# A two-block transformer kernel on one core: gate work, head order and the spatial product rearranged

## The reference, cut to what matters

```
x = first_block(x, ...)      # pool mixer, layer norm, SwiGLU, layer norm
# second block: two layers, each h = h + rmsnorm(mixer(rmsnorm(h)))
# layer 0: differential attention, 8 heads, and a chunked mLSTM, 4 heads
s = where(k_pos <= q_pos, q @ kT, -inf)            # two score maps a head
p = softmax(s); a = p[0] - lam * p[1]; o = a @ v
# mLSTM: log_sigmoid(f), cumulative sums and running maxima over chunks of 128
# layer 1: spatial gating, 8 groups of 256 columns, chunks of 128 tokens
vs = einsum('gts,bcsgd->bctgd', w_spatial * causal, vg) + b_spatial
y = gelu(u) * vs * silu(z);  out = y @ w_out
```

## Time and profile before

| | us |
|---|---|
| Median of 3 runs (2949.52 to 2954.93) | 2954.9 |
| Profiled execution, device time | 2955.26 |
| Its span, first to last instruction | 2953.5 |
| PE busy in it | 2818.0 (95%) |
| PE weight loads busy | 2264.0 (77%) |
| DVE busy | 1359.2 (46%) |
| POOL busy | 1209.1 (41%) |
| ACT busy | 745.6 (25%) |

### The profile page before, as it was taken

The page is one execution under the profiler, slowest core; times in us unless marked ns, Lnnn a source line. Parts: engine busy times, 40 slices in busy tenths (PEclk is TensorE's granted clock), DMA queues, the critical chain, the costliest instruction groups (busy, mean ns, idle before and its releaser), DMA issues.

```text
span 2953.5 us, 38283 instructions
## 1 busy us (share of the span) xinstructions
PE 2818.0 (95%) x14586; PEld 2264.0 (77%) x14586; DVE 1359.2 (46%) x2131; ACT 745.6 (25%) x1218; POOL 1209.1 (41%) x583
## 2 busy tenths in 40 slices
PE   7899999999988899999997999999989999999997
PEld 2588888888867777777775888888778888888885
DVE  6433433343365466555556654645440034444445
ACT  3600000000035333333332222232441322111112
POOL 0544444444335322222221334433254455555555
PEclk9999999999999999999998999999999999999999
DMA  9211111111102100101010111111223311111113
GB/s 386 79 55 45 50 50 43 50 50 45 40 30 87 36 29 28 36 28 36 30 34 15 51 51 50 50 48 52 86 95 106 111 61 57 57 57 57 57 64 122
DMA packets 62900, 185.35 MB, mean 63 GB/s; under 512 B 17108, under 2 KB 23380, under 8 KB 60648
## 3 DMA queue, kind: packets, MB, share of 16 engines
q1 hardware_dynamic: 42016, 152.68, 15.1%
q10 hardware_dynamic: 20808, 31.61, 3.1%
HBM read 163.22 MB, written 21.05 MB: 62 GB/s over the span
## 4 chain that ended last, share of the span: by engine, by line
PE 83%; DVE 7%; ACT 4%; issue 3%; DMA 1%; POOL 1%; DVEq 0%; ACTq 0%; SPq 0%; POOLq 0%
PE ps L711 26%; PE ps L713 25%; PE ps L712 25%; PE ps L1051 2%; DVE acc L2186 1%; PE ps L779 1%; PE ps L1062 1%; DMA resid<-x_t 1%; DVE stat L2337 1%; PE ps L885 1%; PE ps L852 1%; ACT sg_z L1989 1%; DVE da_al L2357 0%; PE ps L1099 0%; ACT ps L1758 0%
## 5 line engine op out<-in xcount | busy, mean ns | idle before, releaser
L538 POOL TENSOR_TENSOR slab_hi<-slab_raw,zero 128x1024 fp32r<-128x1024 f32 x227 | 433.6, 1910 | 1514.8 <-PE ps L713 1408.7
L711 PE MATMUL ps<-h_hi,slab_hi 128*128 128x512 f32 x2256 | 895.4, 397 | 11.8 <-POOL h_lo L554 5.1
L713 PE MATMUL ps<-h_hi,slab_lo 128*128 128x512 f32 x2256 | 883.0, 391 | 0.0
L712 PE MATMUL ps<-h_lo,slab_hi 128*128 128x512 f32 x2256 | 882.4, 391 | 0.0
L540 POOL TENSOR_TENSOR slab_lo<-slab_raw,slab_hi 128x1024 fp32r<-128x1024 f32 x227 | 573.0, 2524 | 17.8
L711 PEld LDWEIGHTS ps<-h_hi,slab_hi 128*128 128x128 f32 x2256 | 425.9, 189 | 111.4 <-issue 14.3
L713 PEld LDWEIGHTS ps<-h_hi,slab_lo 128*128 128x128 f32 x2256 | 425.3, 189 | 91.7
L712 PEld LDWEIGHTS ps<-h_lo,slab_hi 128*128 128x128 f32 x2256 | 426.3, 189 | 84.6
L2186 DVE TENSOR_TENSOR acc<-ps,acc 128x512 f32<-128x512 f32 x352 | 228.7, 684 | 24.5 <-PE ps L713 23.1
L2193 DVE TENSOR_TENSOR ffn_p<-ps,ffn_g 128x1024 f32<-128x1024 f32 x22 | 26.9, 1224 | 454.3 <-PE ps L713 448.7
L2184 DVE SCALAR_TENSOR_TENSOR resid<-ps,mod,resid 128x512 f32<-128x512 f32 x320 | 213.1, 743 | 0.0
(11 more groups left out here) (327 smaller groups left out, 4042.1 us busy)
## 6 DMA issues: line engine op xcount, KB each, us to landing
slab_raw<-w_in SPq DMA_DIRECT2D x168, 512.0 KB, 3.6
mod_big<-mod_w SPq DMA_DIRECT2D x12, 2048.0 KB, 11.2
slab_raw<-w_c SPq DMA_DIRECT2D x43, 512.0 KB, 3.6
res_scr<-resid ACTq DMA_DIRECT2D x4, 2048.0 KB, 7.2
resid<-res_scr ACTq DMA_DIRECT2D x2, 4096.0 KB, 12.9
gv_scr<-sg_t ACTq DMA_DIRECT2D x4, 2048.0 KB, 7.1
slab_raw<-gv_scr SPq DMA_DIRECT2D x16, 512.0 KB, 3.5
resid<-x_t SPq DMA_DIRECT2D x2, 2048.0 KB, 16.1
```

The lines of the kernel that those rows point to most:

```text
L538: pool.tensor_tensor(hi, raw[slot][:], zeros, ALU.add).then_inc(hi_done.sem, 1)
L711: pe.matmul(dst, w_h, r_h, start=first, stop=False, skip_group_check=True)
L712: pe.matmul(dst, w_h, r_l, start=False, stop=False, skip_group_check=True)
L713: return pe.matmul(dst, w_l, r_h, start=False, stop=last, skip_group_check=True)
```

## The change

The spatial weights' high and low parts become one tile of 2 x 8 x 128; a chunk takes one 256-column matmul (the value slab's high part by both) and one 128-column matmul (its low part by the high weights), into 2048 columns of PSUM instead of 1024, and DVE adds the two halves in two passes. `gates(3)` (six of eight chunks) moves into block 0 of head 0, the gate's subtractions on POOL behind one more slab split each for the next head's values and queries, ACT's exponentials ahead of a value copy and the stores behind block 4's exponentials. In the heads, ACT copies block 4's second turned part before the query half and the squares, and the second query half before block 7's exponentials; DVE's order follows. One output addition of block 3 moves between the two maxima. In the norms ahead of attention, tile 2 of half 1 is centred and squared later, and POOL's low split of the slab IN_DA + 1 waits for `mean_square`.

```diff
-        wr_hi, wr_lo = (take(f"sg_{n}", [P, NC, P], F32R)[0] for n in ("wrh", "wrl"))
+        wr_both = take("sg_wrb", [P, 2, NC, P], F32R)[0]
+        wr_hi, wr_lo = (wr_both[:, n, :, :] for n in range(2))
...
+        spatial = ps[:, 2 * T:4 * T].rearrange("p (c h t) -> p c h t", h=2, t=P)
@@ pool: split gets an argument fused, and between its two operations
+                if fused is not None:
+                    pool.wait_ge(n_fuse.sem, fused)
@@
             split_in(IN_DA, 0, IN_DA // 2)
+            split(IN_DA + 1, 1, in_load[1], in_load[1].at((IN_DA + 1) // 2), in_hi, in_mm, in_split, n_fuse.at(0, 2))
             for s in range(1, 8):
-                split_in(IN_DA + s, s % 2, (IN_DA + s) // 2)
+                if s >= 2:
+                    split_in(IN_DA + s, s % 2, (IN_DA + s) // 2)
                 if s == 1:
                     split_low(1, range(2 * KT))
-                if s == 3:
+                if s == 5:
                     gate_exponents()
@@ tensor
                 for c in range(NC):
-                    mm = three(PS[2][:, c * CHUNK:(c + 1) * CHUNK], whi[C][:, c, :], wlo[C][:, c, :],
-                               wr_hi[:, c, :], wr_lo[:, c, :], True, True)
+                    pe.matmul(spatial[:, c, :, :], whi[C][:, c, :], wr_both[:, :, c, :], start=True, stop=False, skip_group_check=True)
+                    mm = pe.matmul(spatial[:, c, 0, :], wlo[C][:, c, :], wr_hi[:, c, :], start=False, stop=True, skip_group_check=True)
@@ scalar: norms
             root_shifted(0)
-            square_centred(1, KT + 2)
             shift(0)
             shift(1)
-            square_centred(1, KT + 3)
+            square_centred(1, KT + 2)
             for k in range(2, KT):
+                split_high(1, k - 2)
+                if k < 7:
+                    square_centred(1, KT + 1 + k)
                 shift(k)
-                split_high(1, k - 2)
-                if k < 6:
-                    square_centred(1, KT + 2 + k)
@@ scalar: gate_rows ends after the exponentials; its wait and five stores are store_gates
@@ scalar: da_head, block i
+                    if i == 6 and not last:
+                        da_q_half(h + 1, 1)
                     if i + 1 < KT:
                         da_exp(h, i + 1)
...
+                    if i in (4, 5):
+                        da_turned(h, i, 1)
+                    if not last and i == 4:
+                        da_q_half(h + 1, 0)
                     if i == 4:
                         da_square(h, 0)
-                    if i == 5:
-                        da_turned(h, i, 1)
...
+                    if i == 2 and first:
+                        gate_rows()
                     if i in (1, 2):
                         da_v_half(h + 1, i - 1)
-                    if not last and i in (4, 6):
-                        da_q_half(h + 1, (i - 4) // 2)
...
-                    if i >= 4 and i != 5:
+                    if i >= 6:
                         da_turned(h, i, 1)
-                    if i == 2 and first:
-                        gate_rows()
+                    if i == 3 and first:
+                        store_gates()
@@ vector: norms
             mean_square(0)
-            center(1, KT + 2)
             gain_first(0)
             reciprocal(2, 0)
             gain_first(1)
-            center(1, KT + 3)
-            gain_first(2)
+            center(1, KT + 2)
             for k in range(KT):
                 layer_input(2, 1, 0, k, "l0_pre_g")
-                if k < 4:
-                    center(1, KT + 4 + k)
                 if k < 5:
-                    gain_first(3 + k)
+                    center(1, KT + 3 + k)
+                if k < 6:
+                    gain_first(2 + k)
@@ vector: da_head
-                        da_max(h, i + 1)
+                        da_max(h, i + 1, (lambda: da_out_add(h - 1, tiles[0], 0)) if out and i == 3 else None)
...
                     if i == 0:
+                        if first:
+                            gates(3)
                         da_turn_low(h, i, 0)
...
-                    if i == 5:
+                    if i in (4, 5):
                         da_turn_low(h, i, 1)
                     if not last and i == 4:
                         da_q_low(h + 1, 0)
...
-            for part in (2, 3):
-                gates(part)
+            gates(2)
             da_k_low(0, 1)
@@ vector: sg_tile, after the first scalar_tensor_tensor, which now reads spatial[:, :, 0, :]
+                dve.wait_ge(e_vs.sem, e_vs.at(d))
+                dve.scalar_tensor_tensor(by_chunk, spatial[:, :, 1, :], gain_col, by_chunk, ALU.mult, ALU.add).then_inc(e_v.sem, 1)
```

More of the change, by code:

```diff
@@ L532, in _, with split @@
             pool.sem_inc(c_split.sem, c_split.prime)
-            def split(n, slot, load, load_value, hi_done, used, done):
+            def split(n, slot, load, load_value, hi_done, used, done, fused=None):
                 pool.wait_ge(load.sem, load_value)
@@ L1660, in gate_rows, with store_gates @@
                 act.activation(g_d3[:], g_d3[:], ACT.Exp).then_inc(g_act.sem, 1)
+            def store_gates():
                 act.wait_ge(g_act.sem, 6)
@@ L2331, in da_out_add, with da_max @@
                 add_half(PS[3], C_DA + h, OUT_DA + h, d, da_halves(d)[n], n=n)
-            def da_max(h, i):
+            def da_max(h, i, between=None):
                 n = (i + 1) * P
                 for c in range(2):
+                    if c == 1 and between is not None:
+                        between()
                     dve.wait_ge(a_score.sem, a_score.at(h, 2 * i + c))
@@ L2420, in da_head @@
                         for d in tiles:
-                            for n in range(2):
+                            for n in range(1 if d == tiles[0] else 0, 2):
                                 da_out_add(h - 1, d, n)
@@ L2659, in sg_tile @@
                 dve.wait_ge(e_yl.sem, e_yl.at(d - 1))
-                dve.scalar_tensor_tensor(sg_v[:].rearrange("p (c t) -> p c t", t=P), PS[2].rearrange("p (c t) -> p c t", t=P),
-                                         par[:, bass.ds(d + COL["sg_g"], 1)],
-                                         bsp[:, bass.ds(g, 1), :].to_broadcast([P, NC, P]), ALU.mult, ALU.add).then_inc(e_v.sem, 1)
+                by_chunk = sg_v[:].rearrange("p (c t) -> p c t", t=P)
+                gain_col = par[:, bass.ds(d + COL["sg_g"], 1)]
+                dve.scalar_tensor_tensor(by_chunk, spatial[:, :, 0, :], gain_col,
+                                         bsp[:, bass.ds(g, 1), :].to_broadcast([P, NC, P]), ALU.mult, ALU.add).then_inc(e_vs.sem, 1)
+                dve.wait_ge(e_vs.sem, e_vs.at(d))
+                dve.scalar_tensor_tensor(by_chunk, spatial[:, :, 1, :], gain_col, by_chunk, ALU.mult, ALU.add).then_inc(e_v.sem, 1)
                 dve.wait_ge(e_v.sem, e_v.at(d))
```

## The result

The changed kernel took 2930.48 us (median of 5 runs, 2925.23 to 2935.02) against 2954.93 us; the ratio is 0.9918, 95% interval 0.9907 to 0.9929. Forecast were 2930.5 us and 2924 to 2938. Timed a second time, beside 2953.48 us for the kernel before, it gave 2934.8 us and 0.9934 (0.9921 to 0.9948); the two medians of one kernel lie 4.3 us apart, and the hit to the tenth is luck. The profiled execution took 2930.48 us (span 2928.7).

What follows compares the result with a forecast made beforehand. PE was taken to bound the kernel, busy 2818.0 of 2953.5 us. Spatial -11.0, heads 1 to 6 -9.6, head 7 -0.9, head 0 -3.5 and norms +0.6 summed to -24.4 us: 2930.5 us, range 2924 to 2938.

Steps and rivals of the forecast that it cites:

- Spatial loop, -11.0: Spatial loop: 0.82 us less in each of 14 tiles, gain of tiles 0 and 1 lost with 0.5 us more; -11.0 us.
- Heads 1 to 6, -9.6: Six loop heads: block 4 gains 0.8, block 6 0.7, the moved addition 0.1; 1.6 us a head, -9.6 us.
- rival 2: Loop heads: gains half absorbed by PE's next wait, 0.8 us a head less; 2935 us, or 2940 if all; chance 0.15.
- (a): Head 0: gate maxima no longer precede the first maximum, so PE's second score map starts at 930.55 instead of 932.42.
- (b): Head 0: moved gate scans meet POOL's split; PE goes on at 942.6, not 940.20, 2.4 us later, after idling 4.5.
- (c): Head 0: lower clock of 1.2 GHz behind the 4.5 us idle stretch, taken as 2.2 us.
- (d): Head 0: gate exponentials and stores moved on ACT; 5.17 us wait shrinks to 0.3, a later one becomes 2.8; -0.9 us.
- (e): Head 0: the two ACT moves, -0.6 and -1.15 us, the last from the 3.13 us wait; lower clock avoided, -0.8.
- Norms, +0.6: Norms ahead of attention: POOL's wait frees the mean 1.0 us earlier, but spread comes later; projection at 869.2, +0.6 us.
- Rival 1: Head 0's opening runs free: scans end before POOL's split or pass it, no lower clock; 2925 us; chance 0.13.
- Rivals 3: Spatial product gains nothing: the 256-column matmul takes two narrow distances; 2942 us; chance 0.04.
- Rival 4: Spatial product slower: the 128-column matmul waits for the wide one's end; 2967 us, deciding from 0.40 us a pair; chance 0.04.

Runs made afterwards that it cites:

- experiment 1: The changed kernel with the old spatial product (24 matmuls of 128 columns, one DVE pass): 2943.59 us, ratio 0.9966.
- Experiment 8: The changed kernel with POOL's split of the second spatial slab ahead of its low part of the first tile: 2925.75 us, ratio 0.9907.
- experiment 4: The changed kernel with all gate work of head 0 in its old places: 2933.03 us, ratio 0.9929.
- experiment 10: The changed kernel itself, unaltered, measured and profiled a second time: 2934.8 us, ratio 0.9934.
- experiment 2: The changed kernel with the old ACT and DVE order in block 4 alone: 2938.18 us, ratio 0.9946.
- 11: The changed kernel with the first output addition behind both maxima of block 4 again, as before: 2932.58 us in one execution.
- Experiment 5: The changed kernel with the old order of centrings, squares, gains and shifts in the norms, POOL's wait for the mean kept: 2932.82 us, ratio 0.993.
- 9: The changed kernel with old norms order, head 0's split behind gate maxima, earlier zeroings, and second spatial slab's split ahead of the low part: 2917.92 us, 0.9881.
- experiment 3: The changed kernel with the second query half behind block 7's exponentials on ACT, as before: 2933.35 us, ratio 0.9928.
- experiment 6: The changed kernel with POOL's split of the next slab in head 0 waiting until DVE's gate maxima are done: 2925.56 us, ratio 0.9905.

## Why the prediction was right

**Spatial loop, -11.0.** Measured 11.1, between first product and end in both experiment 1 and the ledger. A tile gained 0.83 (forecast 0.82). Tiles 0 and 1 together, from product 0 to product 2, took 54.97 us against 54.75: their gain was lost, by 0.2 us and not by 0.5. Experiment 8 shows the chain that I named as the cause. By the formula of the Trainium skill (TensorE: Matmul & The Clock Gate, Back-to-back issue gap) a pair would cost 109 + 56 ns, an estimate. The same section calls it the gap of an isolated matmul, too short for a stream of 128-column matmuls with weight loads, and the trace agrees with that: it shows 230 ns a pair, and removing the product's new form cost 11 us.

**Heads 1 to 6, -9.6.** Measured -9.06, 1.51 a head: block 4 0.79 (forecast 0.8), block 6 0.74 (0.7), the addition -0.1 (0.1). Both waits shrank by 1.85 us, and counting them whole would have promised 11 us: rival 2 names the effect, and the forecast had it in its 0.8.

**Head 7, -0.9.** By its waits 1.0 (5.89 to 4.91), by the ledger 3.8. The rest goes with the clock. The windows over head 7 of before, of the changed kernel, and of the kernel of experiment 4, which has the same head 7:

```profile
1541.00:1646.00 105.00, 84.22 (x402) 66.77 (x401) 67.85 (x105) 28.24 (x53) 16.38 (x8) 0.87 0.10 31
```
```profile
1530.00:1631.00 101.00, 81.27 (x403) 63.70 (x403) 69.03 (x104) 28.13 (x53) 15.90 (x8) 0.92 0.11 32
```
```profile
1532.00:1635.00 103.00, 83.68 (x398) 66.21 (x396) 66.88 (x103) 27.32 (x52) 15.59 (x8) 0.87 0.10 31
```

With equal waits head 7 lasts 100.6 us at 0.92 and 103.5 at 0.87. Behind its first long wait, where PE's list never changes, it takes 66.7 to 67.3 us in four traces and 69.7 to 70.7 in the nine others, the kernel before among them. So the 2.8 us are not shown to come from the change. The forecast had no term for this, nor for the +1.6 us behind it; in the second profiled execution of the changed kernel (experiment 10) that part reads -2.3.

**Head 0, -3.5.** Measured -2.6. (a) exact. (b) 942.43 against 942.6. The Trainium skill (SBUF — State Buffer, SBUF: two separate sides) calls what holds the scans up an exclusive lock for the whole instruction; the trace agrees: 1.72 and 2.65 us, and 0.15 and 0.47 once the split was moved. (c) was 2.7, not 2.2: 24 matmuls from 942.75 took 8.4 us, where such a half takes 5.7. (d) came out 0.2 us late at 960.86.

Three steps of the sum failed. The first is in (d): "and the lower clock that followed it is gone: -0.9". It is gone (0.91 against 0.74 from 955 to 975 us), but from that wait to block 4's second turned part it is 14.29 us, against 14.38 in experiment 4 with the lower clock: DVE's chain sets the end, and PE only waits for it (0.8 us in both). Worth 0.1. The second is in (e): "The two ACT moves as in the loop: -0.6 and -1.15". The first was worth 0.5 us with the gate work moved (experiment 2) and 0.9 without (experiment 4 against the kernel before), the second nothing: the wait stayed at 3.17, as the scaling that starts 2 us earlier ran into POOL's zeroings. The row was in the trace before: the same scaling took 1.46 us there, where it takes 0.74 alone, and I did not ask why.

The third is the clock: "which then should not bring the clock down (0 to -1.6; I take -0.8)". Its reason fell with the wait, and yet from 998.14 to head 1 PE took 24.8 us, before 26.4, twice what I gave. That is the luck of this execution: behind the same wait the kernels of experiments 1 and 11 took 26.4 and 27.5. So the gate work's move is shown to be worth nothing up to 998.14, and of head 0's -2.6 only the first 1.0 is shown to come from the edits. What decides the clock behind that wait stays open.

**Norms, +0.6.** At the projection +0.8. Experiment 5 splits it: -1.0 for the wait, as forecast, and +1.8 for the order, where I had 1.6. By 874 only 0.1 was left (the same matmul starts at 873.99 against 873.89). Before, the whole opening of the projection has starts 0.43 us apart, the 1.2 GHz spacing; after, its first three starts lie 0.31 and 0.23 us apart, and both traces are back at the short spacing by 874. The granted clock from 860 to 890 us was 0.89 before and 0.94 after. Whether the edit did that is open: in the profile of experiment 2, with the same norms, the clock was 1.00 there and PE 1.6 us ahead at 887. The order itself is a loss: from the first spread to the wait at 887 it is 27.6 or 27.7 us in nine of the ten traces with the new order, and 26.8 and 25.6 in the two with the old one (experiments 5 and 9).

**The sum.** The total fits better than its parts deserve: 0.5 and 0.9 us were missed in the heads, and two stretches of clock, -2.8 and +1.6 us, came in uncounted. The kernel's second measurement, 2934.8, lies as far above the forecast as such stretches reach. What experiments 1 to 3 show as caused by the change is the spatial loop and the six loop heads, 20 of the 24 us. Rival 1 was out by the 4.44 us; its price of 5.5 was about right (experiment 6: 6.6 us up to the last long wait, 4.9 at head 1). Rivals 3 and 4 were out by the 0.23 us a pair. Rival 4's limit was miscounted: 13.4 us of other gains are eaten at 0.45 us a pair, not at 0.40.

## What to carry to other kernels

A wait that goes is worth what the next wait in the same chain leaves of it: 1.85 us of waits a head were 1.51 us. Before moving an all-SBUF DVE operation earlier, look at what POOL does in the slot where it lands; here such moves cost 4.4 us of idle PE at one place and the whole expected gain at another, and one semaphore on a POOL operation with slack gave 4.9 us at the next head. Where edits are worth a few us, read them from the distances between fixed places in the trace, up to the last wait that the edit can reach, and look at the same stretch in every trace that shares its instructions: here two executions of one kernel differ by 4 us, and a difference of 1.64 us that matched the forecast lay wholly in a stretch that no edit had touched.

## What the runs showed of the hardware that I had not expected

- Eight POOL zeroings in a row hold up a DVE scaling of one SBUF tile until the last is over. It started 2.0, 0.9 and 0.9 us before their end (changed kernel, experiment 3, kernel before), took 2.56, 1.48 and 1.46 us, and ended 0.5 us behind it each time; alone it takes 0.74.
- A DVE operation on a 4x1 operand was held until POOL's split operation beside it ended: 1.72 us instead of 0.15.
- The granted clock of the same instructions differs between executions (0.93 and 1.00 over 42 us of norms, 0.94 and 1.00 from 860 to 890 us, 1.00 and 0.90 behind one wait of 3.17 us in head 0, where PE then took 24.8 and 27.5 us). What decides it stays open.
- A 256-column and a 128-column matmul in turn cost 0.23 us a pair, the sum of their distances in streams of one form (0.120 and 0.111), even though the second adds to columns that the first has just written.
